# A decoder layer in split precision: a fourth seven-product unit in each up block, sums of weights by adding DMA, and head tokens in pairs

## The chip, the cores and the metric

The kernel runs on one core of a Trainium2 chip. The metric is the device time of one execution in microseconds (us), the median over runs.

## What is computed

One layer of a decoder trunk on 256 tokens of width 2048, in float32: half a step of a gated feed-forward (5504 hidden features), a combined projection into two groups of heads (latent attention, and a gated linear recurrence), an output projection, cross attention to 256 memory tokens, and another half step of feed-forward. Cut to what the change touches:

```python
def swiglu(h, w_gate, w_up, w_down):
    return (jax.nn.silu(h @ w_gate) * (h @ w_up)) @ w_down
...
x = x + 0.5 * swiglu(rmsnorm(x, ffn1_norm), w_gate, w_up, w_down)
...
x = x + 0.5 * swiglu(rmsnorm(x, ffn2_norm), w_gate, w_up, w_down)
```

## The kernel before, in words

**Split products.** Every weight tile (128 x 512) and every token tile is split into a high part and a low part (`w_hi`, `w_lo`, `hT_hi`, `hT_lo`); a product is three matmuls (high x high, low x high, high x low). ScalarE makes the high parts (`hi`, `hi_raw`, `hi_made`: lines 704, 791, 798), VectorE subtracts them for the low parts (`lo`, `lo_parts`: lines 1190, 1261).

**Slots.** SyncE loads weights into a ring of six slots of up to four tiles (`w_raw`; the low parts take the same place). A load waits until the slot six places before is used up (`slot_used`, two counts a slot). High parts have a ring of three slots, so ScalarE follows TensorE by three slots.

**Blocks.** A feed-forward runs over two halves of the hidden features (24 and 19 tiles). In each half, up blocks (`Duo` with `up`) make 4 tiles of hidden features from gate and up weights (16 row tiles; the last block of the second half has 3 tiles, 384 columns), then two down blocks use them, each for two blocks of 512 output columns. The first gate and up pair of each feed-forward is done plainly (`first_pair`), in 8 slots of 4 tiles.

**Units.** Part of a block's rows is done in units: two row tiles, two token tiles and the two column blocks (gate and up, or two output blocks) as a 2 x 2 product in 7 products, not 8. A unit has two slots: the loaded one (2 row tiles of each side) and one of four sums, which VectorE makes from it (`combine`, lines 1244 to 1253: one instruction of two tiles and two of one tile), so that slot has no load. TensorE needs sums of token tiles too (`hS_*`, `aS_*`, made by `token_sums`, split by `sums_hi` and `sums_lo`). Units leave part sums in PSUM, which ScalarE and VectorE take once a block (`first_part`, line 817; `take_parts`, lines 1313 to 1318; line 1315 is executed once in each block). The other rows go through plain slots, one for each side (`firsts`, then `seconds`).

**Order.** All engines follow one order written out by hand: a unit and a plain slot of the first side in turn as long as there are units, then the plain slots of the second side. An up block has units at row tiles 0, 2, 4 and plain slots of 4, 3, 3 tiles; down blocks have 4 units and four slots of 4 (first half), or 3 units and slots of 4, 3, 3, 3 (second half). Activations are turned by TensorE in two rounds a block (`turn_round`), inside the first plain slot and the second unit. VectorE begins a block's later units with `combine`, and their low parts, those of the plain slot, and the takes follow in its queue; the next block's first unit is combined at the end of the block before.

**Head.** `load_first` brings the turned tokens (`xT`) and the first weights: tiles 0 to 3 one by one, then tokens in loads of four tiles (line 528), each with its slot of weights. `first_slots` (lines 901, 890, 704 on ScalarE; 1424, 1190 on VectorE) turns four token tiles into high and low parts, then the weight slot. `flat_first` copies six token tiles for the sums. Line 734 takes the sums of squares, lines 602 and 604 are GpSimd's norm. GpSimd issues no DMA.

Of the kernel before, what the change touches and what calls it, by code (L numbers as in the profile page):

```python
# [16 lines left out]
F32 = mybir.dt.float32  # L17
# [67 lines left out]
class Duo:  # L85
# [5 lines left out]
    width: int  # L91
    units: list
# [4 lines left out]

    def place(self, c):
        for n in range(max(len(self.units), len(self.plains))):
            if n < len(self.units):  # L100
                self.raws.append(c)
                c += 2
            if n < len(self.plains):
# [24 lines left out]
def layer(nc, a, out):  # L128
# [18 lines left out]
    with ctx:  # L147
# [30 lines left out]
        level_mask = sb("level_mask", [P, LEVELS, P], U8)  # L178
        causal = sb("causal", [P, SEQ])
# [72 lines left out]
        hS_hi = at("hS_hi", A0 + 48, [P, 3, 4, P], F32R)  # L252
        hS_lo = at("hS_lo", A0 + 54, [P, 3, 4, P], F32R)
        hS_sum = at("hS_sum", A0 + 54, [P, 3, 4, P])
        aS_hi = at("aS_hi", A0 + 60, [P, 4, 3, P], F32R)
        aS_lo = at("aS_lo", A0 + 66, [P, 4, 3, P], F32R)
        aS_sum = at("aS_sum", A0 + 66, [P, 4, 3, P])
        actT_sum = at("actT_sum", A0 + 24, [P, FA, SEQ])
        flat = [at("flat_0", A0 + 20, [P, 2, SEQ]), at("flat_1", A0 + 22, [P, 2, SEQ]), at("flat_2", A0 + 72, [P, 2, SEQ])]
# [9 lines left out]
        loaded = [sem(f"raw_loaded{s}") for s in range(RAW)]  # L269
        hi_done = sem("hi_done")  # L270
# [10 lines left out]
        xT_in = [sem(f"xT_in{k}") for k in range(4 + 3)]  # L281
# [47 lines left out]
        def number_ffn(f):  # L329
# [3 lines left out]
            for h, (f0, tiles) in enumerate(HALVES):  # L333
                for b in range(1 - h, -(-tiles // 4)):
                    DUOS.append(Duo(f, True, h, b, min(4, tiles - 4 * b) * P, [0, 2, 4], [(6, 4), (10, 3), (13, 3)]))
                for j in range(DB // 2):
                    DUOS.append(Duo(f, False, h, j, NW, *(([0, 2, 4, 6], [(8, 4), (12, 4), (16, 4), (20, 4)]),
                                                          ([0, 2, 4], [(6, 4), (10, 3), (13, 3), (16, 3)]))[h]))
# [64 lines left out]

        GB = {f: blocks[f, "up", 0] % 2 for f in (1, 2)}
        PARTS = [small[:, 0, :], small[:, 1, :], tr[:, 1, :]]
        H_SUMS, A_SUMS = 3, (4, 3)
# [54 lines left out]

        @block.sync
        def _(sp):
# [6 lines left out]

            def rows_of(w, k0, tiles, cols):
                return w[k0 * P:(k0 + tiles) * P, cols].rearrange("(k p) n -> p k n", p=P)

            def load_duos(f):

                wg, wu, wd = (a[f"ffn{f}_w_{n}"][0] for n in ("gate", "up", "down"))
                for m in range(FIRST[f], LAST[f] + 1):
# [13 lines left out]

                    def load_plain(c, side, k, tiles):
# [7 lines left out]
                    for n, (k, tiles) in enumerate(d.plains):  # L500
                        if n < len(d.units):
                            load_unit(d.raws[n], d.units[n])
                        load_plain(d.firsts[n], 0, k, tiles)
# [21 lines left out]
            def load_first():  # L525
# [69 lines left out]
        def _(pool):  # L595
# [47 lines left out]
            done.wait()  # L643
            norm("x1")
            norm("mem")
# [40 lines left out]
            norm("x4")  # L686


        @block.scalar
        def _(act):  # L690
# [3 lines left out]
            def hi(c, rep, tiles, width):  # L694

                c += rep
                for i, (k0, k1) in enumerate(halves(tiles)):
                    if c == 1 and i == 0:
# [3 lines left out]
                    if c >= SPLIT:  # L702
                        act.wait_ge(slot_used, 2 * (c - SPLIT) + i + 1)
# [63 lines left out]
            def flat_x():  # L767

                for n in range(H_SUMS):
# [5 lines left out]
                    if n % 2:  # L775
                        turned_hi(hT_hi, 4 * (n // 2), groups["x_o"] + n // 2, 0, gain=col["ffn2_norm"])
# [9 lines left out]
            def hi_raw(c, width):  # L786

                act.wait_ge(loaded[c % RAW], landed(c))
                for i, (k0, k1) in enumerate(RAW_PARTS):
                    act.wait_ge(slot_used, 2 * (c - SPLIT) + i + 1)  # L790
                    nc.scalar.activation(piece(w_hi, c % SPLIT, k0, k1, width), piece(raw, c % RAW, k0, k1, width), ACT.Copy).then_inc(hi_done, 1)  # L791

            def hi_made(c, n, width):

                for i, (k0, k1) in enumerate(MADE_PARTS):
                    act.wait_ge(ev("combined"), 2 * n + i + 1)
                    act.wait_ge(slot_used, 2 * (c - SPLIT) + i + 1)
                    nc.scalar.activation(piece(w_hi, c % SPLIT, k0, k1, width), piece(raw, c % RAW, k0, k1, width), ACT.Copy).then_inc(hi_done, 1)  # L798

            def turn_round_hi(m, r):  # L800
# [5 lines left out]
                if v < A_SUMS[d.half]:  # L806
                    act.wait_ge(ev("sums_made"), sums_number(m, max(0, v - 2)))
                    nc.scalar.activation(flat[v % 3][:].rearrange("p k t -> p (k t)"), tr[:, 0, :], ACT.Copy)
# [10 lines left out]
            def duos(f):  # L819
# [4 lines left out]
                for m in range(m0, LAST[f] + 1):  # L824
                    d = DUOS[m]
                    u0, u1, w = unit_number(m, 0), len(d.raws), d.width
                    for n, (k, tiles) in enumerate(d.plains):
                        if 0 < n < u1:
                            hi_raw(d.raws[n], w)
                            hi_made(d.raws[n] + 1, u0 + n, w)  # L830
                            if n == 1 and turns_in(d):
                                turn_round_hi(m, 0)
                        hi(d.firsts[n], 0, tiles, w)
                        if n == 1 and turns_in(d):
                            turn_round_hi(m, 1)
                        if n == u1:
                            first_part(m, w)
                    for n, (k, tiles) in enumerate(d.plains):
# [6 lines left out]
                        if n == 0 and u1 == len(d.plains):  # L845
# [1558 lines left out]
```

## Time and profile before

| | |
|---|---|
| median of 3 runs | 1889.87 us (1889.83 to 1889.91) |
| profiled execution | 1891.52 us, span 1889.6 us |
| TensorE, VectorE, ScalarE, GpSimd busy | 99%, 82%, 57%, 5% |
| DMA | 362.55 MB, 192 GB/s, 57% of the 16 engines |

Busy is the share of the span in which an engine worked on some instruction; matmuls are pipelined, so that one of 0.39 us begins every 0.227 us. "Idle before" is an engine's pause, with what ended it. The granted clock of TensorE is given as a share of its full speed. A line number can be that of a helper that many places call.

### The profile page before, as it was taken

What the parts mean: (1) busy time and instruction counts of PE and PEld (TensorE: products, weight loads), DVE (VectorE), ACT (ScalarE), POOL (GpSimd) and SP (SyncE); (2) the same over time, 40 slices, a digit from 0 to 9 for tenths busy, and PEclk for the clock granted to TensorE, in tenths of its full rate; (3) what the DMA queues carried; (4) which work ended last, traced back from release to release, by engine and by line L of the source; (5) the groups of instructions that cost most, each with busy time, mean ns of one, the idle gap of its engine ahead of it and who ended that gap; (6) DMA issues with size and microseconds to landing.
All of it is one profiled execution on the core that took longest, in us unless ns stands there. A gap on an engine that the chain in (4) does not pass through costs nothing.

```text
span 1889.6 us, 23072 instructions
## 1 busy us (share of the span) xinstructions
PE 1877.6 (99%) x8836; PEld 1576.3 (83%) x8836; DVE 1550.7 (82%) x1955; ACT 1077.2 (57%) x1437; POOL 96.6 (5%) x98
## 2 busy tenths in 40 slices
PE   8999999999999999999999999999999999999999
PEld 7888888888889888988888888888888888888987
DVE  6999998888999877655666774689999978899986
ACT  6665555546556547545475655566565554555553
POOL 0000000000000001312250000000000000000000
PEclk9999999999999999999999999999999999999999
DMA  9655565655556674555443654456656665655654
GB/s 328 231 182 192 200 207 200 223 188 195 196 174 209 219 237 154 170 170 179 141 156 105 207 181 153 156 178 200 200 179 203 220 216 174 212 190 185 199 191 171
DMA packets 176862, 362.55 MB, mean 192 GB/s; under 512 B 8048, under 2 KB 19312, under 8 KB 176112
## 3 DMA queue, kind: packets, MB, share of 16 engines
q1 hardware_dynamic: 176464, 360.89, 57.2%
q8 instruction: 70, 1.15, 0.2%
q14 instruction: 40, 0.33, 0.1%
q10 hardware_dynamic: 288, 0.19, 0.0%
HBM read 358.95 MB, written 2.10 MB: 191 GB/s over the span
## 4 chain that ended last, share of the span: by engine, by line
PE 96%; DVE 1%; ACT 1%; DMA 1%; POOL 1%; issue 0%; SPq 0%; DVEq 0%; ACTq 0%; POOLq 0%
PE acc L1889 19%; PE acc L1887 19%; PE acc L1888 19%; PE acc L1876 8%; PE acc L1878 8%; PE acc L1877 8%; PE small L1887 2%; PE small L1889 2%; PE small L1888 2%; PE small L2088 2%; PE tr L1845 1%; PE tr L1889 1%; PE tr L1887 1%; PE tr L1888 1%; PE tr L1903 1%; DMA w_raw<-in_ffn_w_gate 0%
## 5 line engine op out<-in xcount | busy, mean ns | idle before, releaser
L1261 DVE TENSOR_TENSOR w_lo<-w_raw,w_hi 128x1024 fp32r<-128x1024 f32 (+2 forms) x720 | 724.7, 1060 | 66.3 <-ACT w_hi L704 46.7
L704 ACT ACTIVATE w_hi<-w_raw 128x1024 fp32r<-128x1024 f32 (+4 forms) x552 | 513.2, 963 | 167.3 <-PE acc L1889 123.3
L1887 PE MATMUL acc<-w_hi,hT_hi 128*128 128x512 f32 (+1 forms) x920 | 354.9, 386 | 0.0
L1889 PE MATMUL acc<-w_lo,hT_hi 128*128 128x512 f32 (+1 forms) x920 | 353.3, 384 | 0.0
L1888 PE MATMUL acc<-w_hi,hT_lo 128*128 128x512 f32 (+1 forms) x920 | 352.9, 384 | 0.0
L1190 DVE TENSOR_TENSOR w_lo<-w_raw,w_hi 128x1024 fp32r<-128x1024 f32 (+1 forms) x184 | 217.9, 1225 | 60.2 <-ACT w_hi L704 58.8
L798 ACT ACTIVATE w_hi<-w_raw 128x1024 fp32r<-128x1024 f32 (+1 forms) x176 | 182.3, 1044 | 114.0 <-DVE w_raw L1249 59.8
L1887 PE MATMUL acc<-w_hi,actT_hi 128*128 128x512 f32 x548 | 213.9, 390 | 0.0
L1889 PE MATMUL acc<-w_lo,actT_hi 128*128 128x512 f32 x548 | 213.3, 389 | 0.0
L1888 PE MATMUL acc<-w_hi,actT_lo 128*128 128x512 f32 x548 | 213.2, 389 | 0.0
L1889 PEld LDWEIGHTS acc<-w_lo,hT_hi 128*128 128x128 f32 x920 | 172.7, 188 | 32.7
L1887 PEld LDWEIGHTS acc<-w_hi,hT_hi 128*128 128x128 f32 x920 | 172.7, 188 | 32.2 <-DVE stage L1318 0.2
L1888 PEld LDWEIGHTS acc<-w_hi,hT_lo 128*128 128x128 f32 x920 | 172.8, 188 | 31.8
L791 ACT ACTIVATE w_hi<-w_raw 128x512 fp32r<-128x512 f32 (+3 forms) x176 | 142.7, 829 | 94.4 <-PE acc L1889 93.5
L1876 PE MATMUL acc<-w_hi,hT_hi 128*128 128x512 f32 (+1 forms) x480 | 186.7, 389 | 4.5 <-DVE w_lo L1190 3.7
L1878 PE MATMUL acc<-w_lo,hT_hi 128*128 128x512 f32 (+1 forms) x480 | 184.5, 384 | 0.0
L1877 PE MATMUL acc<-w_hi,hT_lo 128*128 128x512 f32 (+1 forms) x480 | 184.2, 384 | 0.0
L1889 PEld LDWEIGHTS acc<-w_lo,actT_hi 128*128 128x128 f32 x548 | 102.9, 188 | 21.5
L1888 PEld LDWEIGHTS acc<-w_hi,actT_lo 128*128 128x128 f32 x548 | 102.9, 188 | 21.3
L1887 PEld LDWEIGHTS acc<-w_hi,actT_hi 128*128 128x128 f32 x548 | 102.9, 188 | 21.2
L1876 PEld LDWEIGHTS acc<-w_hi,hT_hi 128*128 128x128 f32 x480 | 90.2, 188 | 22.2 <-issue 4.5
L1249 DVE TENSOR_TENSOR w_raw<-w_raw 128x1024 f32<-128x1024 f32 (+1 forms) x88 | 105.4, 1198 | 0.0
(306 smaller groups left out, 2547.9 us busy)
## 6 DMA issues: line engine op xcount, KB each, us to landing
w_raw<-in_ffn_w_down SPq DMA_DIRECT2D x68, 1024.0 KB, 5.2
w_raw<-in_w_in SPq DMA_DIRECT2D x36, 1024.0 KB, 5.0
w_raw<-in_ffn_w_gate SPq DMA_DIRECT2D x38, 768.0 KB, 4.3
w_raw<-in_ffn_w_up SPq DMA_DIRECT2D x38, 768.0 KB, 4.4
w_raw<-in_ffn_w_gate SPq DMA_DIRECT2D x56, 512.0 KB, 3.9
w_raw<-in_ffn_w_up SPq DMA_DIRECT2D x54, 512.0 KB, 4.8
w_raw<-in_ffn_w_up SPq DMA_DIRECT2D x26, 1024.0 KB, 5.9
w_raw<-in_ffn_w_gate SPq DMA_DIRECT2D x24, 1024.0 KB, 5.1
```

The source lines that it names most:

```text
L704: nc.scalar.activation(piece(w_hi, c % SPLIT, k0, k1, width), piece(raw, c % RAW, k0, k1, width), ACT.Copy).then_inc(hi_done, 1)
L791: nc.scalar.activation(piece(w_hi, c % SPLIT, k0, k1, width), piece(raw, c % RAW, k0, k1, width), ACT.Copy).then_inc(hi_done, 1)
L798: nc.scalar.activation(piece(w_hi, c % SPLIT, k0, k1, width), piece(raw, c % RAW, k0, k1, width), ACT.Copy).then_inc(hi_done, 1)
L1190: v.tensor_tensor(piece(w_lo, c % RAW, k0, k1, width), piece(raw, c % RAW, k0, k1, width), piece(w_hi, c % SPLIT, k0, k1, width).bitcast(F ...
L1249: v.tensor_tensor(made[:, 0:2, :], b[:, 1:4:2, :], b[:, 0:2, :], ALU.subtract).then_inc(ev("combined"), 1)
L1261: v.tensor_tensor(piece(w_lo, c % RAW, k0, k1, width), piece(raw, c % RAW, k0, k1, width), piece(w_hi, c % SPLIT, k0, k1, width).bitcast(F ...
L1876: mm(dst, xh, wh, start=first and kk == 0, stop=False)
L1877: mm(dst, xl, wh, start=False, stop=False)
L1878: ins = mm(dst, xh, wl, start=False, stop=last and kk == tiles - 1)
L1887: mm(dst, lhs_hi, wh, start=first, stop=False)
L1888: mm(dst, lhs_lo, wh, start=False, stop=False)
L1889: return mm(dst, lhs_hi, wl, start=False, stop=last)
```

## The change

- Up blocks have four units (row tiles 0, 2, 4, 6) and plain slots of 2, 3, 3 tiles. The order is a string: `upupuup` for up blocks (u a unit, p a plain slot of the first side), `upupupup` and `upupupp` for down blocks, as before. All engines walk it by `steps`; `parts_at` says when the part sums are taken; `freed` replaces the wait on half a used slot, since a slot of two tiles counts differently.
- The slot of sums: SyncE loads two tiles of the second side into it, once the slot five places before the unit's first is used up. GpSimd then issues two DMA transfers of one tile each that add to them in SBUF (`add_weights`, after its x1 norm, and after x4 for the second feed-forward). VectorE makes the other two sums by two additions of one tile. Signs of sums are changed to fit. ScalarE's high part of the first two sums waits for the adding transfers.
- At the head the tokens from tile 4 on come in loads of two tiles, one before and one behind the weights; ScalarE and VectorE make half a weight slot after each pair, and TensorE waits for pairs. The third slot's loads wait for an earlier event.
- Token sums are made for four pairs of tiles, with buffers for each; their places in SBUF move.

```diff
-                    DUOS.append(Duo(f, True, h, b, min(4, tiles - 4 * b) * P, [0, 2, 4], [(6, 4), (10, 3), (13, 3)]))
+                    DUOS.append(Duo(f, True, h, b, min(4, tiles - 4 * b) * P, "upupuup", [0, 2, 4, 6], [(8, 2), (10, 3), (13, 3)]))
...
-                fetches[r], fetches[r + 1] = 2 if duo.up else 1, 0
+                fetches[r], fetches[r + 1] = 2 if duo.up else 1, 1
...
-        H_SUMS, A_SUMS = 3, (4, 3)
+        H_SUMS, A_SUMS = 4, (4, 3)
...
+                        sp.wait_ge(slot_used, 2 * (c + 1 - RAW + 1))
+                        made = raw[:, (c + 1) % RAW, :].rearrange("p (k n) -> p k n", k=4)
+                        sp.dma_start(made[:, 0:2, 0:d.width], right_rows(m, k, 2)).then_inc(loaded[(c + 1) % RAW], 16)
...
-                x_tiles(4, 4, xT_in[4])
+                x_tiles(4, 2, xT_in[4])
                 sp.wait_ge(first_in[1], 16)
                 for b, done in enumerate((first_in[4], loaded[1])):
+                    if b:
+                        x_tiles(6, 2, xT_in[5])
...
-                for s in range(2, 4):
-                    sp.wait_ge(xT_in[2 + s], 16)
-                    x_tiles(4 * s, 4, xT_in[3 + s])
+                for s, landed_ in ((2, first_in[3]), (3, loaded[1])):
+                    sp.wait_ge(landed_, 16)
+                    x_tiles(4 * s, 2, xT_in[2 + 2 * s])
                     load(s, 0, rows_of(wg, 4 * s, 4, slice(0, NW)), 4, NW)
+                    x_tiles(4 * s + 2, 2, xT_in[3 + 2 * s])
...
+            def add_weights(f):
+
+                for m in range(FIRST[f], LAST[f] + 1):
+                    d = DUOS[m]
+                    for n, c in enumerate(d.raws):
+                        c += 1
+                        made = raw[:, c % RAW, :].rearrange("p (k n) -> p k n", k=4)
+                        pool.wait_ge(loaded[c % RAW], landed(c))
+                        for i, rows in enumerate((left_rows, right_rows)):
+                            nc.gpsimd.dma_start(made[:, i:i + 1, 0:d.width], rows(m, d.units[n], 1), accum_op=ALU.add).then_inc(added[c % RAW], 16)
+
             norm("x1")
+            add_weights(1)
             norm("mem")
...
                 for i, (k0, k1) in enumerate(MADE_PARTS):
-                    act.wait_ge(ev("combined"), 2 * n + i + 1)
-                    act.wait_ge(slot_used, 2 * (c - SPLIT) + i + 1)
+                    if i == 0:
+                        act.wait_ge(added[c % RAW], summed(c))
+                    else:
+                        act.wait_ge(ev("combined"), 2 * n + 2)
+                    act.wait_ge(slot_used, freed(c, i))
...
                 dve.wait_ge(loaded[c % RAW], landed(c))
-                dve.wait_ge(slot_used, 2 * (c + 1 - RAW + 1))
-                v.tensor_tensor(made[:, 0:2, :], b[:, 1:4:2, :], b[:, 0:2, :], ALU.subtract).then_inc(ev("combined"), 1)
+                dve.wait_ge(added[(c + 1) % RAW], summed(c + 1))
+                v.tensor_tensor(made[:, 2, :], made[:, 1, :], b[:, 0, :], ALU.add).then_inc(ev("combined"), 1)
                 dve.wait_ge(ev("combined"), 2 * n + 1)
-                done(v.tensor_tensor(made[:, 2, :], b[:, 3, :], made[:, 0, :], ALU.subtract))
-                done.wait()
-                v.tensor_tensor(made[:, 3, :], b[:, 2, :], made[:, 2, :], ALU.subtract).then_inc(ev("combined"), 1)
+                v.tensor_tensor(made[:, 3, :], made[:, 2, :], b[:, 2, :], ALU.add).then_inc(ev("combined"), 1)
```

## Rows read from the trace of the kernel before

**Rows 1.** The page: busy time of each engine, and the chain that ended last, by engine.
```profile
PE 1877.6 (99%) x8836; PEld 1576.3 (83%) x8836; DVE 1550.7 (82%) x1955; ACT 1077.2 (57%) x1437; POOL 96.6 (5%) x98
...
PE 96%; DVE 1%; ACT 1%; DMA 1%; POOL 1%; issue 0%; SPq 0%; DVEq 0%; ACTq 0%; POOLq 0%
```

**Rows 2.** Windows view, one up block: width, then busy time of each engine, clock, DMA share.
```profile
208.16:250.63 42.47, 42.47 (x192) 35.12 (x191) 40.37 (x52) 24.19 (x31) 0.00 (x0) 1.00 0.60 198
```

**Rows 3.** Timeline of TensorE in an up block: start, duration, what.
```profile
236.36 0.39 PE L1887 MATMUL small<-w_hi,hT_hi 128*128 128x512 f32 x1
...
237.04 0.39 PE L1887 MATMUL acc<-w_hi,hT_hi 128*128 128x512 f32 x1
...
237.72 0.39 PE L1887 MATMUL acc<-w_hi,hS_hi 128*128 128x512 f32 x1
```

**Rows 4.** The head: a load on the chain, then the timelines of ScalarE and TensorE.
```profile
10.46 8.86 DMA w_raw<-in_ffn_w_gate
...
10.08 1.71 ACT L901 ACTIVATE hT_hi<-xT_raw,gains 128x256 fp32r<-128x256 f32 x4 [0.64 <-DMA xT_raw<-in_x_turned]
...
14.14 0.47 PE L1876 MATMUL acc<-w_hi,hT_hi 128*128 128x512 f32 x1 [1.78 <-DVE w_lo L1190]
...
21.80 0.47 PE L1876 MATMUL acc<-w_hi,hT_hi 128*128 128x512 f32 x1 [1.94 <-DVE w_lo L1190]
```

**Rows 5.** One line's instructions over the span: takes of part sums.
```profile
L1315 DVE TENSOR_TENSOR stage<-tr,stage x28: 558/691/693, 81.2 to 1861.8; 128x512 f32<-128x512 f32 x26, 128x384 f32<-128x384 f32 x2
```

**Rows 6.** Groups by form (busy, mean ns, idle before), and one row of VectorE's timeline.
```profile
L1261 DVE TENSOR_TENSOR w_lo<-w_raw,w_hi 128x1024 fp32r<-128x1024 f32 x494 | 581.1, 1217 | 62.3 <-ACT w_hi L704 42.7 <-ACT w_hi L798 15.6 <-ACT w_hi L791 3.1
...
L798 ACT ACTIVATE w_hi<-w_raw 128x1024 fp32r<-128x1024 f32 x164 | 172.4, 1059 | 108.1 <-DVE w_raw L1249 55.2 <-PE acc L1889 30.2 <-DVE w_raw L1253 18.7
L1261 DVE TENSOR_TENSOR w_lo<-w_raw,w_hi 128x512 fp32r<-128x512 f32 x178 | 121.7, 684 | 1.1 <-ACT w_hi L704 1.1
...
L1249 DVE TENSOR_TENSOR w_raw<-w_raw 128x1024 f32<-128x1024 f32 x82 | 99.7, 1216 | 0.0
...
L1251 DVE TENSOR_TENSOR w_raw<-w_raw 128x512 f32<-128x512 f32 x82 | 56.8, 692 | 2.8
...
L791 ACT ACTIVATE w_hi<-w_raw 128x512 fp32r<-128x512 f32 x82 | 50.9, 620 | 11.0 <-PE acc L1889 10.8
...
232.06 1.21 DVE L1249 TENSOR_TENSOR w_raw<-w_raw 128x1024 f32<-128x1024 f32 x1
```

**Rows 7.** Windows of the head; DMA view of 226 to 268 us (40 slices).
```profile
0.00:10.00 10.00, 8.17 (x43) 7.42 (x44) 4.20 (x9) 5.39 (x10) 0.30 (x5) 1.00 0.78 260
...
30.00:40.00 10.00, 10.00 (x45) 8.27 (x45) 5.87 (x16) 5.94 (x10) 0.00 (x0) 1.00 1.02 395
...
GB/s 27 150 404 183 43 203 406 339 8 0 0 144 396 291 345 402 289 394 242 20 156 402 279 378 402 121 8 0 35 349 412 203 0 59 277 410 254 0 0 0
...
q1 hardware_dynamic: 3744, 8.39, 59.7%
```

**Rows 8.** DMA issues (KB each, us to landing), and all landings of line 487.
```profile
w_raw<-in_ffn_w_gate SPq DMA_DIRECT2D x56, 512.0 KB, 3.9
w_raw<-in_ffn_w_up SPq DMA_DIRECT2D x54, 512.0 KB, 4.8
...
w_raw<-in_ffn_w_gate SPq DMA_DIRECT2D x4, 256.0 KB, 3.8
...
DMA to landing us min/median/max: 3.3/4.3/11.0
```

**Rows 9.** Timelines of ScalarE, VectorE and GpSimd before the first unit.
```profile
46.02 2.00 ACT L704 ACTIVATE w_hi<-w_raw 128x1024 fp32r<-128x1024 f32 x2
...
47.09 2.36 DVE L1190 TENSOR_TENSOR w_lo<-w_raw,w_hi 128x1024 fp32r<-128x1024 f32 x2
49.37 1.22 DVE L1249 TENSOR_TENSOR w_raw<-w_raw 128x1024 f32<-128x1024 f32 x1
...
44.86 0.70 POOL L604 TENSOR_TENSOR rsq<-rsq,minus_half 128x2 f32<-128x2 f32 x1
```

More of the change, by code:

```diff
@@ L91 @@
     width: int
+    order: str
     units: list
@@ L96, with steps, parts_at @@
     seconds: list = field(default_factory=list)
+    def steps(self):
+        return [(kind, self.order[:i].count(kind)) for i, kind in enumerate(self.order)]
+    def parts_at(self):
+        left = self.order[self.order.rindex("u"):].count("p")
+        return ("p", len(self.plains) - left + 1) if left > 1 else ("second", 0)
     def place(self, c):
-        for n in range(max(len(self.units), len(self.plains))):
-            if n < len(self.units):
+        for kind, n in self.steps():
+            if kind == "u":
                 self.raws.append(c)
                 c += 2
-            if n < len(self.plains):
+            else:
                 self.firsts.append(c)
@@ L269, in layer @@
         loaded = [sem(f"raw_loaded{s}") for s in range(RAW)]
+        added = [sem(f"weights_added{s}") for s in range(RAW)]
         hi_done = sem("hi_done")
@@ L459, in layer, with rows_of, columns_of, right_rows @@
         block = ctx.enter_context(nc.Block())
+        def rows_of(w, k0, tiles, cols):
+            return w[k0 * P:(k0 + tiles) * P, cols].rearrange("(k p) n -> p k n", p=P)
+        def columns_of(m, side):
+            d = DUOS[m]
+            f0 = HALVES[d.half][0]
+            n0 = (f0 + 4 * d.block) * P if d.up else (2 * d.block + side) * NW
+            w = a[f"ffn{d.f}_w_{('gate', 'up')[side] if d.up else 'down'}"][0]
+            return w, 0 if d.up else f0, slice(n0, n0 + d.width)
+        def right_rows(m, k, tiles):
+            w, k0, cols_ = columns_of(m, 1)
+            return rows_of(w, k0 + k, tiles, cols_)
+        def left_rows(m, k, tiles):
+            w, k0, cols_ = columns_of(m, 0)
+            return rows_of(w, k0 + k, tiles, cols_)
         @block.sync
@@ L844, in duos @@
                         hi(d.seconds[n], 0, tiles, w)
-                        if n == 0 and u1 == len(d.plains):
+                        if ("second", n) == d.parts_at():
                             first_part(m, w)
@@ L1234, in token_sums @@
                 done.wait()
-                v.tensor_tensor(rest[2], src[:, 1, 0:P], rest[0], ALU.subtract).then_inc(ev("sums_made"), 1)
+                v.tensor_tensor(rest[2], src[:, 1, 0:P], rest[0], ALU.add).then_inc(ev("sums_made"), 1)
             def sums_lo(n, pieces):
@@ L1352, in duos @@
                         take_second(m - 1)
-                    for n, (k, tiles) in enumerate(d.plains):
-                        if 0 < n < u1:
+                    for kind, n in d.steps():
+                        if kind == "u" and n:
                             combine(d.raws[n], u0 + n, w)
@@ L1372, in duos @@
                         lo_parts(d.seconds[n], PLAIN_PARTS[tiles], w)
-                        if n == 0 and u1 == len(d.plains):
+                        if ("second", n) == d.parts_at():
                             take_parts(m)
@@ L2002, in duos @@
                     d, turns = DUOS[m], turns_in(DUOS[m])
-                    for n in range(len(d.plains)):
-                        if n < len(d.raws):
+                    for kind, n in d.steps():
+                        if kind == "u":
                             unit(m, n, (lambda: turn_round(m, 1)) if n == 1 and turns else None)
-                        plain(m, 0, n, (lambda: turn_round(m, 0)) if n == 0 and turns else None)
+                        else:
+                            plain(m, 0, n, (lambda: turn_round(m, 0)) if n == 0 and turns else None)
                     for n in range(len(d.plains)):
```

128 lines of the change are left out of this document (74 added, 54 removed).

## The prediction

> **What bounds the kernel now.** I began with the page's busy times and its chain of waits [rows 1]. TensorE is busy 1877.6 of 1889.6 us and holds 96% of the chain; VectorE comes next with 82%, ScalarE has 57%, GpSimd 5%. So time is won only by taking matmuls away or by closing TensorE's pauses, and there are 12.0 us of pauses in all. Then I cut an up block out of the trace by windows [rows 2]: from one take of the part sums to the next an up block lasts 42.47 us, TensorE is busy in all of it, at a granted clock of 1.00 (the upper level, 2.4 GHz), and VectorE is busy for 40.37 us. The average of 82% hides this: in up blocks VectorE has only 2.1 us to spare. The DMA share there is 0.60 at 198 GB/s. The third view is the order of time in TensorE [rows 3]: the first matmul of one product starts at 237.04, that of the next at 237.72, so a product (three matmuls on split operands) costs 0.68 us; with 384 of 512 columns I count three quarters, 0.51. An up block of 61 products is 41.5 us, and two turns of activations make up the rest, 0.5 us each. The head of the kernel is read the same way [rows 4]: TensorE stands still for 1.78 us before 14.14 and for 1.94 us before 21.80, both times for VectorE's low part of a weight tile, which waited for ScalarE, which waited for tokens from memory.
>
> **The change, part by part.**
>
> *Products.* A unit covers two row tiles, two token tiles and two column blocks in 7 products, where plain slots need 8. An up block goes from 3 units and 10 plain tiles a side (21 + 40 = 61 products) to 4 units and 8 tiles a side (28 + 32 = 60). There are ten up blocks in each feed-forward, 20 in all (the 28 takes of part sums are 20 up and 8 down [rows 5]), of which two have 384 columns. Removed: 18 x 0.68 + 2 x 0.51 = 13.3 us of a TensorE that is the chain. Down blocks keep their products.
>
> *VectorE.* A unit's three combining instructions (1.22 + 0.69 + 0.69 = 2.60 us, the third as large as the second [rows 6]) become two of 0.69. In an up block that is 4 x 1.38 in place of 3 x 2.60, -2.3 us. The low parts of an extra unit take 0.68 + 3 x 1.22 = 4.3 us [rows 6]; the plain slots lose a 4-tile slot against a 2-tile one on each side, -2 x 1.07 = -2.1 us. Sum -0.1 us: VectorE stays at 40.3 us, now of 41.8, so its room shrinks from 2.1 to 1.5 us. In down blocks it is relieved by 28 x 1.2 us, which is worth nothing, since TensorE is always busy there. ScalarE gets 0.62 + 3 x 1.06 us for the unit and loses 2 x 0.88 on the plain slots, +2.0 us [rows 6] on 24.2 of 42.5: hidden.
>
> *Bytes.* An up block moves 8.39 MB now [rows 7]. Each unit adds two tiles loaded by SyncE and two added by GpSimd, 1.05 MB, so it becomes 12.58 MB in 41.8 us, 301 GB/s. The head shows what the queue can do: 395 GB/s between 30 and 40 us with a share of 1.02 [rows 7]. So 301 fits, with much less slack between bursts. Set against that is the Trainium skill, Collectives: The Full Stack, section on the bandwidth ceiling: an add in the DMA engines reads two sources, which doubles the read traffic of each byte. By it the adding 2.1 MB would count twice and the block would ask for 352 GB/s, still under 395; no row here shows an adding transfer.
>
> *The new wait.* This is the uncertain part. Until now VectorE made a sum slot from the loaded slot alone. Now the slot of sums is first loaded by SyncE (512 KB, once the slot five places before the unit's first is used up), then GpSimd waits for the landing and issues two adding transfers of 256 KB, and VectorE's first combining instruction waits for both. VectorE works in order: behind that wait stand the unit's own low parts and all of the plain slots after it, and TensorE waits for those. How long may the chain take? In the new order (unit, plain, unit, plain, unit, unit, plain, then three plains of the other side, with 2, 3 and 3 tiles) TensorE works, between the release and the third unit, through plain 2, a unit, plain 3: 4 + 7 + 6 products = 11.6 us and two turns, 12.6 (most of the second). VectorE needs its adds and the first low part before the unit starts (2.1 us), and since the fourth unit follows at once it must be about 3.3 us ahead: 9.3 us are left. The fourth unit and the second have 17 products and one turn, 12.1 us, and need 2.7 (adds, first low part, and half of the second), which leaves 9.4 us. Today's lead confirms the scale: combining starts at 232.06 for a unit that TensorE reaches at 236.36 [rows 3, 6]. In down blocks the gap is over 14 us; nothing is lost there.
>
> What the chain takes: a 512 KB load lands after 3.9 us (median), 4.8 when it stands behind its twin, at best 3.3; a 256 KB load took 3.8 [rows 8]. No row shows a transfer issued by GpSimd. Bounds: two adding transfers together cost no less than the quickest 512 KB load, 3.3, and no more than two full 512 KB landings one after the other, 9.6. I take 3.8 for the first and 0.5 for the second behind it, nearest to the row of the same size: 0.1 + 3.9 + 0.1 + 4.3 = 8.4 us, between 6.7 and 14.6. With 8.4 under 9.3 the wait costs TensorE nothing, but the cover is 1 us thin. If it is gone by x us, two of the waits in a block pay (the third is lengthened by the pause before it): 2x a block, 40x in all. The Trainium skill, DMA: Bandwidth & Descriptors, section on the anatomy of a GpSimd-issued DMA, gives 2.0 us fixed and the bytes at 436 GB/s; by an estimate from that page the pair would take about 3.2 us and the chain 7.3.
>
> *The head.* Tokens come in pairs of tiles, each ahead of its weights, and ScalarE makes half a weight slot after each pair. The two pauses are 3.7 us together. For the first, two token tiles (0.85 us) in place of four (1.7) stand before the weights [rows 4], so it may nearly close; the second depends on when the third slot lands, 8.86 us after its issue at 10.46. But what is won must pass the eighth slot: ScalarE squares the residual, then makes the token sums' high parts (now four, +0.55 us) and only at 46.02 the slot's high part [rows 9]; the low part starts at 47.09 and its first half is ready at 48.3, while TensorE, from slot 2 at 21.80 with five slots of 8 products between, comes at 49.0. The first 10 us leave the DMA about a fifth idle [rows 7], so the loads before it can come 1 to 2 us sooner. Bounds 0 and -3.7; I take -1.0. The first unit's adds must wait for GpSimd's x1 norm, done at 45.6 [rows 9]; plus 4.3 that is 49.9, beside 49.4 for the combining today, and this combining is 1.2 us shorter: nothing, at worst +1. In the second feed-forward the norm comes first too, long before its adds.
>
> **Sum.** -13.3 - 1.0 = -14.3 us. The profiled execution took 1891.52 us with a span of 1889.6; the median of the runs is 1889.87, so the difference is taken from the median: 1875.5 us. Its own range: the head's pauses closed and a little more 1871.5, and up to 5 us of small waits back, 1881.
>
> **Rivals.**
> - *The adding chain is late* (slower, 0.28). With every step at its loaded value, the load behind a twin 4.8 and the pair 4.8 + 0.8, the chain takes 10.6 us, x is 1.2 over 9.4, and 20 x 2.4 = 48 us come on top: 1923.5. It decides at x = 0.36, a chain of 9.8 us. For it: bursts above 400 GB/s already [rows 7], half as many bytes again, three queues in series. Against it: the queue idles 40% of a block, and each pause of TensorE lengthens the next window.
> - *The saving is mostly eaten* (within 0.2%, 0.12). VectorE's room of 1.5 us a block is used up by late sums and semaphore steps; 0.5 to 0.9 us a block is lost, 10 to 18 us, and the time is 1886 to 1893.
> - *The doubled reads fill the queue* (part of the slower chance, 0.05). If an adding byte costs three plain ones or more, a block needs 12.58 + 2 x 2.1 = 16.8 MB, at 395 GB/s 42.5 us against 41.8, and with the bursts' waits several us a block: 1950 or more.
> - *More than forecast* (part of the faster chance, 0.05): the head's pauses close, -3.7 in place of -1.0, and with what other pauses of the 12.0 us go, 1871.5 to 1873.
>
> **Numbers.** About 0.2% (3.8 us) is what a measurement of this kernel can tell from no change. Faster 0.60, same 0.12, slower 0.28. The range must reach into the slower cases until two in ten are left: 1871 to 1912.
>
> **What would show it.** Right: 60 products and about 41.8 us between takes of an up block; TensorE busy in all of it; VectorE's combining waits on DMA for under 1.5 us a block; adding transfers landing within about 4.5 us; down blocks unchanged in length. Wrong: TensorE pauses ended by VectorE's low parts before the second and fourth unit, VectorE idle until w_raw's DMA, a DMA share near 1 in up blocks. The head is right if slot 2 starts about 1 to 2 us before 14.14 and the first unit about 1 us sooner. A 512 KB or adding landing above 5 us would make the forecast wrong.

## The result and the profile after

The changed kernel takes 2149.53 us (median of four runs, 2147.3 to 2153.31) where the kernel before takes 1889.89 (1889.83 to 1890.47): a ratio of 1.1372, interval 1.1357 to 1.1386. Forecast were 1875.5 us and a range of 1871 to 1912. The time is 274 us above the forecast and outside the range.

The page of the changed kernel: busy times and the shares of the chain that ended last, as in [rows 1], then what the queues carried (q1 is SyncE's, q0 GpSimd's) and the loads' time from issue to landing.

```profile
span 2149.9 us, 23550 instructions
PE 1965.7 (91%) x8776; PEld 1599.7 (74%) x8776; DVE 1515.8 (71%) x1997; ACT 1108.9 (52%) x1523; POOL 286.6 (13%) x314
...
q1 hardware_dynamic: 206912, 416.47, 57.4%
q0 software_dynamic: 31104, 55.59, 15.7%
...
PE 56%; DMA 30%; DVE 7%; issue 3%; POOL 2%; SPq 1%; ACT 1%; DVEq 0%; ACTq 0%; POOLq 0%
...
w_raw<-in_ffn_w_up SPq DMA_DIRECT2D x162, 512.0 KB, 5.7
...
w_raw<-in_ffn_w_gate POOLq DMA_DIRECT2D x72, 256.0 KB, 5.5
w_raw<-in_ffn_w_up POOLq DMA_DIRECT2D x72, 256.0 KB, 7.2
```

TensorE has 60 recorded matmuls fewer, which are the 18 products of full and 2 of three-quarter width that were to go, yet is busy 88.1 us longer, and its pauses grew from 12.0 to 184.2 us. DMA went from 1% of the chain [rows 1] to 30%. SyncE's loads of two tiles from `w_up`, 4.8 us before [rows 8], take 5.7 (those from `w_gate` 4.4 for 3.9), and GpSimd's second adding transfer lands 7.2 us after its issue. The list of waits (engine, tile and line, what it waited for: us in total, times, longest) names the transfer into the slot of sums and what stands behind it:

```profile
DVE w_raw L1320 <- DMA w_raw<-in_ffn_w_up: 189.0, 57, 8.8
...
PE small L1964 <- DVE w_lo L1330: 159.8, 68, 7.7
...
DVE w_raw L1320 <- DMA w_raw<-in_ffn_w_down: 123.9, 21, 11.0
```

L1320 is VectorE's first combining instruction, L1330 the low parts, L1964 TensorE's first matmul of a unit. The window of one up block has the columns of [rows 2]:

```profile
142.84:194.88 52.04, 45.48 (x189) 35.14 (x188) 40.06 (x55) 30.18 (x39) 7.02 (x8) 0.97 0.85 243
```

It lasts 52.04 us, where 42.47 were measured before and 41.8 forecast. VectorE's work is as forecast (40.06 us for 40.3); the time went into waiting. One chain, that of a block's third unit, on the timelines of SyncE, GpSimd, VectorE and TensorE (start, duration, what, and in brackets the pause before it):

```profile
165.53 0.46 SPq L537 DMA_DIRECT2D w_raw<-in_ffn_w_up  x1
...
172.36 0.86 POOL L704 DMA_DIRECT2D w_raw<-in_ffn_w_gate  x1 [11.82 <-DMA w_raw<-in_ffn_w_up]
172.90 1.21 POOL L704 DMA_DIRECT2D w_raw<-in_ffn_w_up  x1
...
181.36 0.69 DVE L1320 TENSOR_TENSOR w_raw<-w_raw 128x512 f32<-128x512 f32 x1 [5.24 <-DMA w_raw<-in_ffn_w_up]
...
183.44 0.79 PE L1964 MATMUL small<-w_hi,hT_hi 128*128 128x512 f32 x1 [3.52 <-DVE w_lo L1330]
184.03 0.63 PE L1965 MATMUL small<-w_hi,hT_lo 128*128 128x512 f32 x1
184.45 0.63 PE L1966 MATMUL small<-w_lo,hT_hi 128*128 128x512 f32 x1
...
187.17 0.40 PE L1964 MATMUL tr<-w_hi,hS_hi 128*128 128x512 f32 x1
187.41 0.39 PE L1965 MATMUL tr<-w_hi,hS_lo 128*128 128x512 f32 x1
```

From SyncE's issue to VectorE's instruction are 15.8 us: 6.8 until GpSimd can issue, 9.0 from there until both tiles have been added. That chain was forecast at 8.4 us with room for 9.3. The last lines show a second loss: behind the pause of 3.52 us matmuls begin 0.42 us apart, TensorE's lower level (1.2 GHz), and only some 3.5 us later about 0.23 apart again (2.4 GHz).

The 260.3 us between the two spans are thus 172.2 more of pauses and 88.1 more of busy time. Taking the 13.3 us of removed products into account, the matmuls that are left cost about 101 us more. By the trace's record of the clock 163 us of the span were granted at the lower level, and TensorE was busy in 131 of them, so about 65 us were lost in that way. The other 36 us or so lie at the upper level, with 144 pauses in place of 13. A matmul record of 0.39 us counts as busy to its end where a pause follows, and the first record behind a pause is about 0.50 us long; how the 36 us divide was not worked out.

Which of a block's waits pay can be counted in the trace. The table has, for the four units of the 20 up blocks in their order, the chain from SyncE's issue to the later landing of GpSimd's two transfers (median), and TensorE's pauses just before the unit's first matmul (sum over the 20 blocks). Number 2 is an experiment below.

| | unit 1 | unit 2 | unit 3 | unit 4 |
|---|---|---|---|---|
| the change, chain, us | 11.7 | 12.1 | 14.8 | 14.5 |
| the change, pauses, us | 9.3 | 13.9 | 77.7 | 4.4 |
| number 2, chain, us | 9.1 | 9.5 | 12.2 | 10.9 |
| number 2, pauses, us | 1.4 | 0.8 | 41.1 | 0.6 |

The third unit pays, and its chain is also the longest. Over all 80 chains of up blocks the median is 13.2 us and the shortest 9.7, so that not one fits into 9.3. The 28 units of down blocks add 52 us of such pauses.

### The profile page after: what moved, and what is told of

The parts are those of the page before. It is cut to its first block, busy times and chain, and to the rows that moved or that the text cites. A ratio compares the mean times of both kernels' runs of the same rounds, so it can differ in the third digit from the quotient of the medians.

```text
span 2149.9 us, 23550 instructions
## 1 busy us (share of the span) xinstructions
PE 1965.7 (91%) x8776; PEld 1599.7 (74%) x8776; DVE 1515.8 (71%) x1997; ACT 1108.9 (52%) x1523; POOL 286.6 (13%) x314
## 3 DMA queue, kind: packets, MB, share of 16 engines
q0 software_dynamic: 31104, 55.59, 15.7%
## 4 chain that ended last, share of the span: by engine, by line
PE 56%; DMA 30%; DVE 7%; issue 3%; POOL 2%; SPq 1%; ACT 1%; DVEq 0%; ACTq 0%; POOLq 0%
DMA w_raw<-in_ffn_w_up 21%; DMA w_raw<-in_ffn_w_down 9%; PE acc L1964 8%; PE acc L1966 8%; PE acc L1965 8%; PE acc L1953 7%; PE acc L1955 7%; PE acc L1954 7%; DVE w_lo L1330 4%; PE small L1964 2%; DVE w_raw L1320 2%; PE small L1966 1%; PE small L1965 1%; PE small L2165 1%; PE tr L1915 1%
## 5 line engine op out<-in xcount | busy, mean ns | idle before, releaser
L1330 DVE TENSOR_TENSOR w_lo<-w_raw,w_hi 128x1024 fp32r<-128x1024 f32 (+3 forms) x800 | 760.6, 1007 | 48.8 <-ACT w_hi L770 43.7
L770 ACT ACTIVATE w_hi<-w_raw 128x1024 fp32r<-128x1024 f32 (+4 forms) x552 | 475.9, 900 | 144.7 <-PE acc L1966 104.1
L867 ACT ACTIVATE w_hi<-w_raw 128x1024 fp32r<-128x1024 f32 (+1 forms) x216 | 223.3, 1041 | 351.7 <-DMA w_raw<-in_ffn_w_up 180.8
L1964 PE MATMUL acc<-w_hi,hT_hi 128*128 128x512 f32 (+1 forms) x800 | 317.8, 397 | 6.0 <-DVE w_lo L1330 5.5
L1966 PE MATMUL acc<-w_lo,hT_hi 128*128 128x512 f32 (+1 forms) x800 | 312.2, 390 | 0.0
L1965 PE MATMUL acc<-w_hi,hT_lo 128*128 128x512 f32 (+1 forms) x800 | 311.7, 390 | 0.0
L1320 DVE TENSOR_TENSOR w_raw<-w_raw 128x512 f32<-128x512 f32 (+1 forms) x108 | 73.5, 680 | 313.4 <-DMA w_raw<-in_ffn_w_up 189.0
L857 ACT ACTIVATE w_hi<-w_raw 128x512 fp32r<-128x512 f32 (+1 forms) x216 | 171.8, 825 | 109.4 <-PE acc L1966 108.4
L1964 PE MATMUL acc<-w_hi,actT_hi 128*128 128x512 f32 x548 | 217.8, 397 | 1.1 <-DVE w_lo L1330 1.1
L1964 PEld LDWEIGHTS acc<-w_hi,hT_hi 128*128 128x128 f32 x800 | 152.0, 190 | 52.7 <-DVE w_lo L1330 20.0
L704 POOL DMA_DIRECT2D w_raw<-in_ffn_w_gate x80 | 69.7, 871 | 886.0 <-DMA w_raw<-in_ffn_w_up 885.8
L1955 PE MATMUL acc<-w_lo,hT_hi 128*128 128x512 f32 (+1 forms) x480 | 184.5, 384 | 0.0
L1954 PE MATMUL acc<-w_hi,hT_lo 128*128 128x512 f32 (+1 forms) x480 | 184.2, 384 | 0.0
L1964 PE MATMUL small<-w_hi,hT_hi 128*128 128x512 f32 (+1 forms) x80 | 38.4, 480 | 105.2 <-DVE w_lo L1330 105.1
L1964 PEld LDWEIGHTS acc<-w_hi,actT_hi 128*128 128x128 f32 x548 | 104.6, 191 | 26.2 <-DVE w_lo L1330 3.7
```

The lines of the kernel that those rows point to most:

```text
L1320: v.tensor_tensor(made[:, 2, :], made[:, 1, :], b[:, 0, :], ALU.add).then_inc(ev("combined"), 1)
L1330: v.tensor_tensor(piece(w_lo, c % RAW, k0, k1, width), piece(raw, c % RAW, k0, k1, width), piece(w_hi, c % SPLIT, k0, k1, width).bitcast(F ...
L1954: mm(dst, xl, wh, start=False, stop=False)
L1955: ins = mm(dst, xh, wl, start=False, stop=last and kk == tiles - 1)
L1964: mm(dst, lhs_hi, wh, start=first, stop=False)
L1965: mm(dst, lhs_lo, wh, start=False, stop=False)
```

## The experiments

The letters are those of the expectations. Theory B: the chain load, landing, two adding transfers is too long for the order of the work, and TensorE waits for it. Rivals: A, it is the adding that is dear; C, the added traffic fills the DMA engines; D, transfers issued by GpSimd cost too much by themselves; E, the fourth unit by itself overloads VectorE's room. Each edit is against the changed kernel unless said otherwise, and each ratio is against the kernel before, timed beside it.

**1. All four sums made by VectorE, no load or adding transfer for that slot.** The first two sums are made by one instruction again, as before the change.

```diff
-                        sp.dma_start(made[:, 0:2, 0:d.width], right_rows(m, k, 2)).then_inc(loaded[(c + 1) % RAW], 16)
...
-            add_weights(1)
...
-                dve.wait_ge(added[(c + 1) % RAW], summed(c + 1))
+                dve.wait_ge(slot_used, 2 * (c + 1 - RAW + 1))
+                v.tensor_tensor(made[:, 0:2, :], b[:, 1:4:2, :], b[:, 0:2, :], ALU.add).then_inc(ev("combined"), 1)
```

> Four units a block as changed, but the slot of sums is made by VectorE from the loaded slot (three instructions, as before), no load and no adding transfer for it. If the adding chain is the whole cause, the loss of 260 us goes away but VectorE becomes the bound in up blocks: 40.3 + 4 x 1.22 = 45.2 us against 41.8, 20 blocks x 3.4 = 68 us above 1873, so 1930 to 1945. If the order of two units in a row or the smaller plain slots were the cause, it stays above 2050.

Measured: 1963.98 us, 1.0388 (1.0372 to 1.0403). Its up block:

```profile
222.60:269.50 46.90, 43.83 (x190) 33.97 (x189) 44.73 (x59) 26.06 (x35) 0.00 (x0) 1.00 0.54 179
```

That is 19 us above the 1945 at which the expectation ended; a block takes 46.9 us, not 45.2. VectorE is busy 44.73 of 46.90 us: four units with VectorE's own sums don't fit under 41.8 us of products. So the change's idea, taking sums off VectorE, was needed for the fourth unit. But 186 of the 260 us go when the transfers go; they cost more than what they relieve.

**2. GpSimd's transfers plain.** The same two transfers write in place of adding; the sums are left out of what is computed.

```diff
-                            nc.gpsimd.dma_start(made[:, i:i + 1, 0:d.width], rows(m, d.units[n], 1), accum_op=ALU.add).then_inc(added[c % RAW], 16)
+                            nc.gpsimd.dma_start(made[:, i:i + 1, 0:d.width], rows(m, d.units[n], 1)).then_inc(added[c % RAW], 16)
```

> GpSimd's two transfers a unit are plain copies over the loaded tiles instead of adds (so the sums are not sums); same waits, same issue, a third less read traffic. Theory A, the adding itself is dear (read twice, slow landing): the chain shortens by 3 us or more, time 1880 to 1980. Theory B, the chain of three queues is too long whatever the transfer does: 2080 to 2140. Theory C, the DMA engines are full: bytes drop from 14.7 to 12.6 MB counted, 1950 to 2050.

**3. Only the load left.** No transfer by GpSimd; VectorE and ScalarE wait for SyncE's load alone. The added tiles are left out.

```diff
-            add_weights(1)
...
-                dve.wait_ge(added[(c + 1) % RAW], summed(c + 1))
+                dve.wait_ge(loaded[(c + 1) % RAW], landed(c + 1))
```

> GpSimd issues nothing; VectorE and ScalarE wait for SyncE's load of two tiles alone (the adds are left out). All theories: most of the loss is gone, 1871 to 1885 if a block of 10.5 MB and a chain of one load fit under 9.3 us. Above 1900 would say that already the load behind the slot five places before comes too late.

**4. The adds aside.** GpSimd issues the same adding transfers at the same landings, into two tiles that nobody waits for; the other waits are as in 3. To make place, the fourth unit uses the third's token sums.

```diff
-                            nc.gpsimd.dma_start(made[:, i:i + 1, 0:d.width], rows(m, d.units[n], 1), accum_op=ALU.add).then_inc(added[c % RAW], 16)
+                            nc.gpsimd.dma_start(aside[i][:, :, 0:d.width], rows(m, d.units[n], 1), accum_op=ALU.add).then_inc(ev("aside"), 16)
```

> GpSimd issues the same two adding transfers a unit after the same load, but into two tiles aside for which nobody in the units waits; the slot keeps its two loaded tiles, and the fourth unit of an up block uses the third's token sums (so its sums are left out). Same traffic, no chain. Theory B (length of the chain): 1875 to 1900, with landings of adds as long as in the changed kernel. Theory C (full DMA engines): at least 2000, since the loads of all slots come late too. Theory A says nothing of this one beyond B.

Measured: number 2 takes 2010.14 us, 1.0636 (1.0617 to 1.0654); number 3 1885.13, 0.9971 (0.9959 to 0.9982), the upper end of what was expected; number 4 1889.63, 0.9993 (0.9983 to 1.0002). Two lines of the page of number 2, then two of the page of number 4 and its up block:

```profile
q0 software_dynamic: 17024, 55.59, 8.1%
...
w_raw<-in_ffn_w_gate POOLq DMA_DIRECT2D x72, 256.0 KB, 3.8
w_raw<-in_ffn_w_up POOLq DMA_DIRECT2D x72, 256.0 KB, 4.6
```

```profile
q0 software_dynamic: 31104, 55.59, 17.6%
...
w_raw<-in_ffn_w_up SPq DMA_DIRECT2D x162, 512.0 KB, 6.8
...
1311.30:1353.80 42.50, 42.45 (x190) 34.61 (x189) 40.21 (x55) 26.12 (x35) 7.10 (x8) 1.00 1.02 304
```

Number 2 fell between the ranges of A and B and inside that of C, so by itself it decided nothing. Number 4 settles C as the main cause: with every byte of the change moving, the DMA engines are full in the block shown (1.02 at 304 GB/s), loads land after 6.8 us, and TensorE works through 42.45 of 42.50 us. (There each pair of adds also waits for the pair before it, which held GpSimd back 21 times.) It is the wait that costs, 260 us. With the adding traffic but without the wait, number 4 is 4.5 us slower than number 3. The adds do double the work of the engines: 55.59 MB took 15.7% of 2149.9 us in the changed kernel, 338 us (17.6% of 1887.0, 332 us, here), and as plain transfers 8.1% of 2009.6, 163 us: a factor of 2.04 to 2.07. Number 2 shows that the chain is too long even without the adding: 0.1 + 5.0 + 0.5 + 4.6 = 10.2 us, over the room of 9.3 (load by load the median is 10.0, from 6.7 to 16.3). Theory A is right in part: making the same transfers plain takes 139 of the 260 us off, with landings of 4.6 us in place of 7.2.

**5. The head alone.** The kernel before, with the tokens in pairs of tiles as in the changed kernel, and nothing else.

```diff
-                x_tiles(4, 4, xT_in[4])
+                x_tiles(4, 2, xT_in[4])
...
+                    if b:
+                        x_tiles(6, 2, xT_in[5])
```

> The kernel before with the head's part of the change alone (tokens in pairs). With the loads alone, TensorE's two head pauses of 1.78 and 1.94 us had shrunk to about 1.4 and 0.0; here 2 to 3.5 us should be won, 1886.5 to 1888. The rival of the prediction, that the gain is taken back at the eighth slot, gives 1889 to 1890.

Measured: 1888.49 us against 1890.44 beside it, 0.9987 (0.9978 to 0.9996), between the two ranges of the expectation. TensorE's pauses, 1.78 and 1.94 us in [rows 4], are on its timeline

```profile
13.01 0.51 PE L1891 MATMUL acc<-w_hi,hT_hi 128*128 128x512 f32 x1 [0.58 <-DVE w_lo L1198]
...
18.94 0.50 PE L1891 MATMUL acc<-w_hi,hT_hi 128*128 128x512 f32 x1 [0.15 <-DVE w_lo L1198]
```

The medians differ by 2.0 us. (The span is 2.9 us shorter than that of before, whose profiled execution was itself 1.6 above its median.) This kernel computes all that the reference does and is the only such version here that beats both kernels, by 0.1%.

**6. One hop.** GpSimd makes a plain load itself as soon as the slot is free; SyncE's load is left out, and so are the adds.

```diff
-                        pool.wait_ge(loaded[c % RAW], landed(c))
+                        pool.wait_ge(slot_used, 2 * (c - RAW + 1))
```

> Four units a block; GpSimd itself makes the plain load of the slot of sums, one tile by each of two transfers, straight after the slot is free; SyncE's load and the adds are left out. Same waits of VectorE and ScalarE. If the chain's length is the cause, one transfer in place of two in series brings back what the run with SyncE's load alone had: 1883 to 1895. If it is GpSimd's queue as such (issue, landing), it stays above 1950.

Measured: 1884.86 us, 0.9969 (0.9957 to 0.9981); the pair lands 3.7 and 4.1 us after its issue. D falls: GpSimd's queue is as quick as SyncE's. What hurts is two landings in series.

**7. One adding transfer in place of two.** SyncE loads one tile, VectorE makes the other three sums.

```diff
-                        for i, rows in enumerate((left_rows, right_rows)):
+                        for i, rows in enumerate((left_rows,)):
...
+                done(v.tensor_tensor(made[:, 1, :], b[:, 1, :], b[:, 3, :], ALU.add))
```

> One adding transfer a unit: SyncE loads one tile, GpSimd adds one, VectorE makes the other three sums (one 0.69 us instruction more). Chain: landing of 256 KB about 4.5, issue and landing of the add about 6, 10.5 to 11.5 us in place of 15 to 16; threshold 9.4. Pause of 1 to 2 us, twice a block, partly without a drop of the clock, and VectorE at 43 us a block: 1930 to 1990. If the second add costs nothing beside the first, it stays at 2100 or more.

Measured: 1990.61 us, 1.0523 (1.0498 to 1.0548), at the upper end of what was expected. The chain falls to 4.0 + 0.1 + 4.7 = 8.8 us, but VectorE has one more instruction a unit, and up blocks mostly take 45 to 46.4 us. A mixture of both bounds, worse than number 1; it separates nothing by itself.

**8. The adds in down blocks only.** Up blocks as before the change: three units, sums by VectorE.

```diff
-"upupuup", [0, 2, 4, 6], [(8, 2), (10, 3), (13, 3)]
+"upupup", [0, 2, 4], [(6, 4), (10, 3), (13, 3)]
...
-                fetches[r], fetches[r + 1] = 2 if duo.up else 1, 1
+                fetches[r], fetches[r + 1] = (2, 0) if duo.up else (1, 1)
```

> Up blocks have three units with VectorE's sums as before; adding transfers are used in down blocks alone (28 units of 108), where TensorE has 14.2 to 15.6 us between the release and the unit. The prediction said that nothing is lost there: 1886 to 1890. In the changed kernel the chain took 14 to 19 us there too and single blocks grew by 8 to 12 us: by that 1915 to 1960. With less traffic in the up blocks nothing else differs.

Measured: 1959.42 us, 1.0359 (1.0343 to 1.0375). Up blocks are back at 42.6 us, and the loss sits where the prediction had said "nothing is lost there". Its waits, then the landings of SyncE's loads into the slot of sums (L539) and of GpSimd's adding transfers (L708):

```profile
DVE w_raw L1332 <- DMA w_raw<-in_ffn_w_down: 117.2, 24, 8.8
...
DMA to landing us min/median/max: 3.5/6.4/9.2
...
DMA to landing us min/median/max: 3.5/6.6/10.1
```

Of 28 units in down blocks 24 kept VectorE waiting, 4.9 us on average. Against number 5, which has the same head, the 28 chains cost 71 us.

**9. Adding transfers, one hop.** GpSimd clears both tiles (0.96 us) and issues two adding transfers at once, with no load before them. SyncE's tiles are missing in the sums.

```diff
-                        pool.wait_ge(loaded[c % RAW], landed(c))
+                        pool.wait_ge(slot_used, 2 * (c - RAW + 1))
+                        done(nc.gpsimd.memset(made[:, 0:2, 0:d.width], 0.0))
```

> Four units a block; SyncE's load of the slot of sums is left out, GpSimd clears the two tiles itself (about 1 us) and then issues the same two adding transfers, so both tiles hold one weight tile and not a sum. The chain is 0.1 + 1 + 0.6 + a landing of 5.5 to 7 us, 7.2 to 8.7 in place of 13.6, under the 9.3 of room. If the length of the chain is what costs, adding transfers on the chain are nearly free: 1884 to 1900. If an add on the chain costs more than its landing (by slowing the loads of the other slots), 1950 or more.

Measured: 1910.13 us, 1.0099 (1.0084 to 1.0114), landings of 4.3 and 6.6 us in up blocks. The chain is 1.3 + 0.5 + 6.6 = 8.4 us: by chance the length that was forecast. Yet the time is 25 us above number 6 and outside the expected 1884 to 1900. Up blocks take 42.3 to 44.0 us, and about half of the loss lies in stretches that hold a down block. So a median of 8.4 us under a room of 9.3 was not free: VectorE's first combining instruction still waited for a transfer 22 times in up blocks (28.5 us) and 8 times in down blocks (14.1 us). The single chains of up blocks run from 6.2 to 10.9 us, 20 of the 80 over 9.3; that it is these that cost is argued from this spread.

**10. Three units, adds everywhere.** Undoes the fourth unit alone.

```diff
-"upupuup", [0, 2, 4, 6], [(8, 2), (10, 3), (13, 3)]
+"upupup", [0, 2, 4], [(6, 4), (10, 3), (13, 3)]
```

> The fourth unit is undone: up blocks have units at 0, 2, 4 and plain slots of 4, 3, 3 tiles, with adding transfers everywhere and the new head. Room before each unit is 14.3 us and a turn, less 2.7, about 12 us, and the chain some 13.5 us: pauses of 1 to 2 us where two waits in a block pay, most too short or too few for a long drop of the clock. Down blocks cost 70 us as in the run with adds there alone; up blocks 20 x 2 to 4 us: 2000 to 2040. If the two units in a row, and not the chain, were what hurts up blocks, only the down blocks' part stays: 1955 to 1965.

Measured: 2068.48 us, 1.0942 (1.0924 to 1.096), blocks of about 48 us, landings 5.3, then 6.2 and 7.7. That is over the 2000 to 2040 expected. E falls as the main cause: against number 5, which has the same head, the adds cost 180 us without the fourth unit. The changed kernel stands 261 us over number 5. Of the difference of 81 us, 41 would be there if each of its 20 further chains cost as much as the other 88 do here (an estimate: 180 x 20 / 88). For the rest, that the third unit has less cover because the fourth follows it at once is argued from the order and the pauses, and was not tried apart.

**11 and 12. Where the 41.8 us are.** Number 11 is number 3 with two of VectorE's instructions at the take of part sums left out besides; number 12 leaves the same two out of number 5, as a control.

```diff
-                done(v.tensor_tensor(nat[:, 0, 0:w], p6, gate[:, 0, 0:w], ALU.add))
-                done.wait()
-                done(v.tensor_tensor(gate[:, 1, 0:w], p7, nat[:, 0, 0:w], ALU.add))
```

> The kernel with SyncE's load alone (no adds, 1885.1 us, up blocks of 42.3 us where 60 products and two turns make 41.8) with two of the four instructions of a take of part sums left out: VectorE has 1.4 us less to do in each block, and nothing else moves. If VectorE's lack of room eats the saved product there, up blocks come down to about 41.8 us, 1875 to 1880. If a fixed cost of TensorE does (new order, turns), it stays at 1884 to 1886.

> Control: the kernel before with the new head (1888.5 us) and the same two instructions left out. Its up blocks show TensorE busy throughout, so less work for VectorE should give nothing: 1887 to 1889.

Measured: 1876.09 us, 0.992 (0.9904 to 0.9937), and 1888.63, 0.9988 (0.9979 to 0.9997). One up block each of number 3 and number 11:

```profile
208.00:250.30 42.30, 42.26 (x190) 34.44 (x189) 39.91 (x55) 26.09 (x35) 0.00 (x0) 1.00 0.73 248
```

```profile
207.00:248.80 41.80, 41.80 (x190) 34.60 (x189) 38.69 (x52) 26.58 (x35) 0.00 (x0) 1.00 0.77 253
```

With 1.2 us taken off VectorE the block is 41.80 us long, as counted from the products, and the whole kernel takes 1876.09. The control gains nothing (1888.63 for 1888.49), so the 9.0 us between number 3 and number 11 are the fourth unit's own, hidden until then behind VectorE.

The chains put together, each as 0.1 us, the median landing of the load if there is one, 0.5 us between the two issues and the landing of the second transfer, against the length of an up block:

| kernel | chain, us | up block, us |
|---|---|---|
| 6, plain, one hop | 4.7 | 42.3 |
| 9, adds, one hop | 8.4 | 42.3 to 44.0 |
| 2, plain, two hops | 10.2 | 46.4 |
| the change | 13.5 | 51.5 |

A longer chain goes with a longer block in every row, but not by the prediction's 9.3 us alone: number 9 is under it and already has blocks of up to 44.0 us, and number 2 is 0.9 us over it and 4.1 us a block longer than number 6.

## Why the prediction was wrong

The step that failed is the price of the new wait. The prediction took 8.4 us for the chain; the medians of the changed kernel make 0.1 + 5.7 + 0.5 + 7.2 = 13.5. Both main terms were too small: the load 5.7 for 3.9, the pair 7.7 for 4.3. The bounds did hold it (6.7 to 14.6), so the fault was the choice among them. The 3.9 was the row of `w_gate`; the slot's load is one of `w_up`, which took 4.8 in the same rows, and the rest came with the new traffic, a block's share of 0.85 for 0.60. The adding pair was priced as a plain load: plain it lands after about 0.5 + 4.6 = 5.1 us behind a load (number 2), adding after 7.7. The late rival went to 10.6 and no further, and the range ended at 1912 though the bound of 14.6, by the prediction's own rule, is 2 x 5.3 x 20 = 212 us.

**The rule that turned lateness into time** came near in the changed kernel, partly by luck. It gives 2 x (13.5 - 9.3) = 8.4 us for an up block, and 9.7 came on top of 41.8. But the prediction let two waits of a block pay, those of the second and the fourth unit, and spared the third; the third has 77.7 of the 105.3 us of pauses. For number 2 the rule gives 1.8 us a block, and 4.6 came on top of 41.8; for number 9 it gives nothing, and that kernel is 25 us over number 6. Its input was one chain for all units, where the third unit's is above the median of all (14.8 for 13.2 us in the change, 12.2 for 10.0 in number 2) and single chains spread by several us. The clock was not in the sum either: in the block shown it is 0.97 over 52.04 us, so about 3.4 us were at half speed and 1.7 us lost.

**"In down blocks the gap is over 14 us; nothing is lost there"** was wrong by 71 us in number 8. The gap was counted from TensorE's work alone, and the chain was held to be 8.4 us. The trace of number 8 has the 28 chains: 14.1 us in the median from SyncE's issue to both adds, 10.7 to 19.4, with landings of 6.4 us for the load and 6.6 for the adding transfers. From a gap of 14.2 to 15.6 us (the expectation of number 8) VectorE's own 2.7 us, as in up blocks, leave 11.5 to 12.9, an estimate; most chains are longer. With 20 x 9.7 = 194 us in up blocks that makes 265 of the 274 us that were missed.

**VectorE's room.** "VectorE stays at 40.3 us" was right. The rival in which its last 1.5 us are eaten was true as well: number 3 has 42.3 us a block and 1885.1 in all, number 11 41.8 and 1876.1. So a chain that nobody waits for would have brought 1885 us (number 3, without the adding transfers) or 1889.6 (number 4, with them, and no clear gain over the kernel before: 0.9983 to 1.0002), and not the forecast's 1875.5. That rival's 1886 to 1893 lies about there.

**Products and head.** The 13.3 us were right: number 11 against number 12, which differ in the fourth unit and in who makes the sums, is 12.5 us. The head gave 2.0 us between medians, not 1.0, inside the bounds; the eighth slot didn't take it back.

**Traffic.** 301 GB/s was forecast, and 304 flowed in the block of number 4 with TensorE busy for 42.45 of 42.50 us. The Trainium skill, Collectives: The Full Stack, section on the bandwidth ceiling, says that an add reads two sources and so doubles the read traffic. The measured factor is of engine time, not of reads, and at 2.04 to 2.07 it is in line with that; the rival that wanted three times or more is out. The prediction asked only whether the queue would fill; it should also have asked what a landing takes in a fuller queue. The other rule, the Trainium skill, DMA: Bandwidth & Descriptors, section on the anatomy of a GpSimd-issued DMA, gives 2.6 us for 256 KB (an estimate from its 2.0 us and 436 GB/s). The runs disagree: medians of 3.7 and 4.1 us plain (number 6), 5.5 and 7.2 adding.

## What to carry to other kernels

A wait made of two landings in series is priced at the traffic that the change itself creates, not at that of the trace before, and its bound at the upper end belongs in the range with the rule that turns it into time. A median under the room is not enough either: take the chain of the unit with the least cover, and the late ones among its landings (number 9). Here a second landing in series made the difference: GpSimd's plain transfers by themselves (number 6) cost nothing, behind a landing (number 2) 6% of the time. And before a unit of work is added, compare the second engine's room in that stage with what its queue needs between the new waits; here 1.5 us of room were too few by half a microsecond a block.

## What the runs showed of the hardware

- An adding transfer to on-chip memory takes about twice the DMA engine time of a plain one of the same bytes (338 and 332 us for 163). GpSimd is busy longer issuing it, too: 0.87 us, and 1.22 for the second of a pair, where the plain ones take 0.55.

```profile
L704 POOL DMA_DIRECT2D w_raw<-in_ffn_w_gate x80: 853/870/1051, 41.7 to 1999.0; - x80
L704 POOL DMA_DIRECT2D w_raw<-in_ffn_w_up x80: 872/1222/1262, 42.5 to 1999.5; - x80
...
DMA to landing us min/median/max: 3.7/6.3/10.9
```

- These lines are of L704 in the changed kernel (ns, minimum, median, maximum). Its landings spread from 3.7 to 10.9 us. An adding 256 KB landed after 6.6 us behind its twin even without a load before it (number 9), a plain one after 4.1 (number 6).
- DMA engines with a share of 1.02 through whole blocks cost little while no wait hung on the added transfers (number 4: TensorE busy 42.45 of 42.50 us in such a block, 4.5 us more than number 3 over the whole kernel), though a load of two tiles from `w_up` then took 6.8 us in place of 4.6 (number 3, share 0.73).
- TensorE's clock fell to its lower level (1.2 GHz) beside single pauses of 2.27, 2.39 and 3.52 us in the changed kernel, with matmuls 0.43 us apart for a time, and not after one of 1.40 us; but two of 2.10 and 2.57 us had no such stretch beside them, so these runs give no limit. Through such stretches a late wait is paid for a second time, here with some 65 us in all (163 us at the lower level, TensorE busy in 131 of them).
